# Delta rule of a five-layer kernel: block inverse in 64-column form, three series steps for two joins, small transposes on VectorE

## The reference, cut to what matters

```python
L = jnp.where(strict, jnp.einsum('bhnid,bhnjd->bhnij', k_beta, k) * decay, 0.0)
A = jnp.eye(C, dtype=L.dtype) + L
rhs = jnp.concatenate([v_beta, k_beta * jnp.exp(g)[..., None]], axis=-1)
sol = lax.linalg.triangular_solve(A, rhs, left_side=True, lower=True)
...
def step(state, xs):
    v_new = u_c - jnp.einsum('bhck,bhkv->bhcv', w_c, state)
    o = (jnp.einsum('bhck,bhkv->bhcv', q_c * jnp.exp(g_c)[..., None], state)
         + jnp.einsum('bhij,bhjv->bhiv', a_c, v_new))
    state = state * jnp.exp(g_last)[..., None, None] + jnp.einsum('bhck,bhcv->bhkv', k_dec, v_new)
```

## Time and profile before

| | us |
|---|---|
| median of 3 runs | 2543.03 (2540.28 to 2546.37) |
| the profiled execution | 2544.22 |
| its span, first to last instruction | 2542.4 |
| TensorE busy in the span | 2493.2 |
| VectorE, ScalarE, GpSimd busy | 1619.2, 1032.0, 1181.5 |
| one middle head, from G row to G row | 64.56 |

### The profile page before, as it was taken

The page is one execution under the profiler, slowest core; times in us unless marked ns, Lnnn a source line. Parts: engine busy times, 40 slices in busy tenths (PEclk is TensorE's granted clock), DMA queues, the critical chain, the costliest instruction groups (busy, mean ns, idle before and its releaser), DMA issues.

```text
span 2542.4 us, 31888 instructions
## 1 busy us (share of the span) xinstructions
PE 2493.2 (98%) x11934; PEld 1995.9 (79%) x11934; DVE 1619.2 (64%) x2722; ACT 1032.0 (41%) x1620; POOL 1181.5 (46%) x1447
## 2 busy tenths in 40 slices
PE   8999999999999999999999999999999998999999
PEld 6888878888888877777777788887888776877777
DVE  5644666666666654444343566546998996577876
ACT  3222254444444353333333332224544667454543
POOL 5665643333333265333344366666554533544432
PEclk9999999999999999999999999999999999999999
DMA  3223221111111132222222122232222211221111
GB/s 136 104 100 108 92 79 53 56 54 58 59 67 48 53 111 82 73 73 80 70 83 77 61 100 93 90 108 101 93 98 77 73 46 50 93 93 67 59 67 42
DMA packets 59721, 198.54 MB, mean 78 GB/s; under 512 B 7089, under 2 KB 9649, under 8 KB 59569
## 3 DMA queue, kind: packets, MB, share of 16 engines
q1 hardware_dynamic: 56688, 192.90, 21.7%
q10 hardware_dynamic: 2880, 3.61, 0.6%
HBM read 192.03 MB, written 2.10 MB: 76 GB/s over the span
## 4 chain that ended last, share of the span: by engine, by line
PE 81%; DVE 13%; ACT 4%; issue 2%; DMA 0%; SPq 0%; ACTq 0%; DVEq 0%
PE psum L327 21%; PE psum L329 20%; PE psum L328 20%; DVE psum L935 4%; PE psum L1812 3%; PE psum L2638 1%; PE psum L2623 1%; DVE e_c L935 1%; DVE e_stg L1102 1%; PE psum L2641 1%; PE psum L3099 1%; PE psum L1818 1%; ACT whi L289 1%; PE psum L3076 1%; PE psum L2614 1%
## 5 line engine op out<-in xcount | busy, mean ns | idle before, releaser
L304 POOL TENSOR_TENSOR wlo<-raw,whi 128x256 fp32r<-128x256 f32 x1436 | 1181.0, 855 | 1334.6 <-ACT whi L289 1334.3
L327 PE MATMUL psum<-xh,whi 128*128 128x512 f32 x1800 | 740.7, 412 | 2.6 <-DVE e_stg L1102 1.8
L289 ACT ACTIVATE whi<-raw 128x1024 fp32r<-128x1024 f32 (+1 forms) x369 | 379.4, 1032 | 803.8 <-PE psum L329 779.9
L329 PE MATMUL psum<-xh,wlo 128*128 128x512 f32 x1800 | 705.5, 392 | 0.0
L328 PE MATMUL psum<-xl,whi 128*128 128x512 f32 x1800 | 704.1, 391 | 0.0
L327 PEld LDWEIGHTS psum<-xh,whi 128*128 128x128 f32 x1800 | 340.3, 189 | 78.1 <-issue 13.9
L329 PEld LDWEIGHTS psum<-xh,wlo 128*128 128x128 f32 x1800 | 339.2, 188 | 73.5
L328 PEld LDWEIGHTS psum<-xl,whi 128*128 128x128 f32 x1800 | 340.1, 189 | 69.9 <-issue 6.9
L523 DVE TENSOR_TENSOR xT<-psum,xT 128x512 f32<-128x512 f32 x232 | 156.1, 686 | 159.9 <-PE psum L329 151.9
L615 DVE TENSOR_TENSOR pool_u<-psum,R 128x512 f32<-128x512 f32 x32 | 22.1, 692 | 132.2 <-PE psum L329 132.2
L327 PE MATMUL psum<-pool_y,whi 128*128 128x512 f32 x256 | 99.6, 389 | 0.0
(11 more groups left out here) (555 smaller groups left out, 4425.1 us busy)
## 6 DMA issues: line engine op xcount, KB each, us to landing
raw<-weights_dram SPq DMA_DIRECT2D x329, 512.0 KB, 3.2
raw<-weights_dram SPq DMA_DIRECT2D x40, 384.0 KB, 2.8
xin<-x_dram SPq DMA_DIRECT2D x4, 512.0 KB, 7.8
mla_xrot<-sq ACTq DMA_DIRECT2D x32, 64.0 KB, 2.0
out_dram<-xT SPq DMA_DIRECT2D x8, 256.0 KB, 2.0
g_masks<-gdn_masks_dram ACTq DMA_DIRECT2D x1, 384.0 KB, 3.6
par<-params_dram SPq DMA_DIRECT2D x1, 327.5 KB, 4.2
mwork<-positions_dram ACTq DMA_DIRECT2D x1, 256.0 KB, 2.8
```

Source lines behind the costliest of these rows:

```text
L289: act.activation(whi[:, q, 0:nk * nm * P], raw[:, q, 0:nk * nm * P], ACT.Copy).then_inc(hi_ready[q], 1)
L304: last = pool.tensor_tensor(wlo[:, q, part], raw[:, q, part], whi[:, q, part].bitcast(F32), ALU.subtract)
L327: pe.matmul(gbank(b), whi[:, q, c:c + P], h, start=k == 0, stop=False)
L329: done = pe.matmul(gbank(b), wlo[:, q, c:c + P], h, start=False, stop=k == nk - 1)
```

## The change

For each chunk the diagonal 64 x 64 blocks of all matrices are kept one above the other, 128 rows by 64 columns ("compact"), for use as the moving operand. The left operand of each product stays a 128 x 128 matrix with two diagonal blocks (`left[0..3]`). P (powers) and V (the growing inverse) lie side by side in one tile, so that one weight load serves P*P and P*V. After the 16 x 16 blocks are inverted, X = V*(N above the 16-blocks) is nilpotent, and V + XV + X^2(..) replaces joins 16 and 32. The left operands are made by VectorE transposes of 32-row blocks (`turn`), read from PSUM or SBUF, 30 instructions a head. The 64-join stays.

TensorE's fours a head go from 10 between kk and the 64-join (kq aside) to 7: P2, P4, P8, PV8, X, X2, X2V, of which P2, PV8, X and X2V have 64 columns each. The five groups of transposes in the inverse go.

Other edits: k dec moves from VectorE (one instruction) to ScalarE (four); the k tokens of the next head are made at the end of a head, behind the pieces of `o 3`; the scale beta/|k|^2 is done ahead of d; the Ln of k stands beside the Ln of o, and 1/rms of o is done in the next head behind exp G row (one Ln and one Exp table load less a head); V0 of the next head is projected and taken ahead of z; five tiles are set to zero once. ScalarE's copies of N2, N4, N8 and of U transposed (two of three) go. Pieces: 8 after kk, 3 after each of the next five steps, and for head 0 none after `o 3`.

```diff
-                four_transposes(0, N, "N transposed")
-                more("N transposed")
-                pe.wait_ge(*ve.of(f"{i} Nt"))
-                four(2, NB[:, 0], N, "N2")
+                pe.wait_ge(*ve.of(f"{i} P"))
+                four(2, left[0], Pw, "P2", 64)
...
+                four(0, left[1], PU, "P4")
+                more("P4")
...
+                pe.wait_ge(*ve.of(f"{i} V2"))
+                four(1, left[0], PU, "P8")
+                more("P8")
+                pe.wait_ge(*ve.of(f"{i} V4"))
+                four(2, left[1], V, "PV8", 64)
+                more("PV8")
+                pe.wait_ge(*ve.of(f"{i} V8 turned"))
+                pe.wait_ge(*ve.of(f"{i} above"))
+                four(0, left[0], Nt, "X", 64)
+                more("X")
+                pe.wait_ge(*ve.of(f"{i} X"))
+                four(1, left[2], PU, "X2")
+                more("X2")
...
+                pe.wait_ge(*ve.of(f"{i} V32"))
+                four(2, left[3], V, "X2V", 64)
...
+                if i < H - 1:
+                    k_tokens(pe, i + 1)
                 pe.wait_ge(*ve.of(f"{i} o summed"))
...
+            def turn(dve, i, name, src, dst, spread_out, blocks):
+                for at_row, at_col in blocks:
+                    to = dst[rows(at_col), :, rows(at_row) if spread_out else cols(at_row)]
+                    last = dve.transpose(to, src(at_row, at_col))
+                last.then_inc(*ve.done(f"{i} {name} turned"))
...
+                turn(dve, i, "N", lambda to, of: N[rows(to), :, rows(of)], Nt, False, [(g, g) for g in range(4)])
+                dve.tensor_tensor(left[0][:, :, :], N[:, :, :], over(bd16), ALU.mult).then_inc(*ve.done(f"{i} N 16"))
+                dve.wait_ge(*ve.of(f"{i} N turned"))
+                dve.tensor_tensor(Pw, Nt[:, :, :], over(in16), ALU.mult).then_inc(*ve.done(f"{i} P"))
+                dve.wait_ge(*ve.of(f"{i} P"))
+                dve.tensor_tensor(V, Pw, over(one64), ALU.add).then_inc(*ve.done(f"{i} V1"))
...
+                turn(dve, i, "P2", lambda to, of: half(2)[rows(to), :, cols(of)], left[1], True, [(g, g) for g in range(4)])
+                dve.wait_ge(*ve.of(f"{i} V1"))
+                dve.tensor_copy(Pw, half(2)).then_inc(*ve.done(f"{i} P2"))
...
+                turn(dve, i, "X", lambda to, of: half(0)[rows(to), :, cols(of)], left[2], True,
+                     [(0, 0), (2, 2), (0, 1), (2, 3), (1, 1), (3, 3)])
+                dve.tensor_copy(Pw, half(0)).then_inc(*ve.done(f"{i} X"))
...
+            EARLY = [8, 3, 3, 3, 3, 3, 2, 2, 2, 3]
+            PIECES = {i: EARLY + [2] * 6 + [1] * 4 + [5] for i in (1, 2, 3, 4)}
+            PIECES[0] = [8, 3, 3, 3, 3, 3, 3, 2, 2, 2] + [2] * 6 + [1] * 4 + [0]
```

More of the change, by code:

```diff
@@ L1781, in behind_vector @@
                     yield from take_and_taps(dve, QQ, i + 1)
+                    yield from take_and_taps(dve, V0, i + 1)
                 for d in range(2):
@@ L1940, in work_scalar, with k_dec @@
                 last.then_inc(*ae.done(f"{i} k squares"))
+            def k_dec(act, i):
+                for c in range(NCH):
+                    last = act.activation(kdec[:, c, :], wbank(0)[:, c * P:(c + 1) * P], ACT.Copy,
+                                          scale=gcol[:, 3, c, i:i + 1])
+                last.then_inc(*ae.done(f"{i} k dec"))
+            def work_scalar(act, i):
+                hi = [in_at(i, V1)]
+                if i < H - 1:
+                    hi += [in_at(i + 1, K), in_at(i + 1, QQ), in_at(i + 1, V0)]
+                hi += [z_at(i, 0), z_at(i, 1)]
+                hi += [at["out", h, x] for h, x in halves[i]]
+                if i == 0:
+                    k_squares(act, 0)
+                    act.wait_ge(*ae.of("exp last-G"))
+                    k_dec(act, 0)
+                    act.wait_ge(*ae.of("0 k squares"))
+                    act.activation(rln, ssk, ACT.Ln, bias=bias[:, 0:1]).then_inc(*ae.done("0 ln k"))
                 act.wait_ge(*ve.of(f"{i} d max"))
@@ L2028, in work_vector @@
                     y_before(1)
-                fill("N2")
-                dve.wait_ge(*te.of(f"{i} U2"))
-                dve.wait_ge(*ve.of(f"{i} U1"))
-                dve.tensor_tensor(U[:, :, :], U[:, :, :], chunks(wbank(1)), ALU.add).then_inc(*ve.done(f"{i} U2"))
+                fill("P2")
+                dve.wait_ge(*te.of(f"{i} P4"))
+                turn(dve, i, "P4", lambda to, of: chunks(wbank(0))[rows(to), :, cols(of)], left[0], True,
+                     [(g, g) for g in range(4)])
@@ L2033, in work_vector @@
+                fill("V2")
+                dve.wait_ge(*te.of(f"{i} P8"))
+                turn(dve, i, "P8", lambda to, of: chunks(wbank(1))[rows(to), :, cols(of)], left[1], True,
+                     [(g, g) for g in range(4)])
+                add_to_v(dve, i, chunks(wbank(1))[:, :, 64:P], "V2", "V4")
                 dve.wait_ge(*ae.of(f"{i} E1"))
@@ L2037, in work_vector @@
                 dve.tensor_tensor(A[:, :, :], chunks(wbank(3)), d1[:, :, :], ALU.mult).then_inc(*ve.done(f"{i} A"))
+                dve.wait_ge(*te.of(f"{i} PV8"))
+                add_to_v(dve, i, half(2), "V4", "V8")
+                dve.wait_ge(*ve.of(f"{i} V8"))
+                turn(dve, i, "V8", lambda to, of: V[rows(to), :, cols(of)], left[0], True, [(g, g) for g in range(4)])
                 dve.wait_ge(*ae.of(f"{i} exp G row"))
@@ new lines, in work_vector @@
+                fill("V32")
+                dve.wait_ge(*te.of(f"{i} X2V"))
+                dve.wait_ge(*ve.of(f"{i} V32"))
+                for h, part in enumerate((HI, LO)):
+                    dve.tensor_tensor(U[part, :, part], V[part], half(2)[part], ALU.add)\
+                       .then_inc(*ve.done(f"{i} U" if h else f"{i} U low"))
+                v_beta(dve, i, 0)
+                fill("U")
+                dve.wait_ge(*te.of(f"{i} join"))
+                dve.tensor_copy(Y[LO, :, LO], quarter(0)).then_inc(*ve.done(f"{i} Y"))
@@ L3709 @@
 BIASES = (EPS, EPS * 128, math.pi / 2, 1e-5, EPS * EPS, 128 * EPS * EPS, 64 * EPS)
-GDN_MASKS = ("upper", "-strict lower", "blocks 16", "join 16", "join 32", "join 64")
+GDN_MASKS = ("upper", "-strict lower", "blocks 16", "compact 16", "compact above", "compact identity")
 def constants():
```

257 lines of the change are left out of this document (113 added, 144 removed).

## The result

The changed kernel takes 2579.36 us in the median of four runs (2576.62 to 2580.49), the kernel before 2543.04 beside it: a ratio of 1.014, interval 1.0128 to 1.0152. It is 36 us slower, where 2532 us, 11 us faster, was forecast; the time lies above the range.

The account below looks back on a forecast made before the run. TensorE was taken to bound the kernel, VectorE having least room. Heads 2 to 7 -10.3, head 0 +3.3, head 1 -6.4 made -13.4 us; less 1.2 to the median, plus 2 for small waits: 2532 us, range 2515 to 2556.

Parts of the forecast that it names:

- the head's start: From the sum of o to P: TensorE asks for P at 10.0 us, VectorE has it at 12.1.
- The wait at P2: TensorE waiting for P at a head's start: 2.1 us lost in place of 0.92 at N.
- the clock behind it: TensorE's granted clock after the wait for P: expected to stay at 1.00; a drop costs about 1.4 us.
- the two ends of the stage: Zeroing of new tiles was to fall into an idle VectorE stretch ahead of the stage; no loss was counted.
- three signs of being wrong: Waits at P2 and X2 under 1 us together; transposes at 0.3 or more; TensorE waiting for weights in the stage.
- passes: TensorE's inverse: three fours, five transpose groups and four changes to pieces fewer, saving 4.9 us a head.
- wait at X2: TensorE waiting for X: VectorE ready at 17.2 us after P, TensorE at 15.7, so 1.5 a head.
- P4, P8, PV8: Small waits at the middle products of the inverse, put at nothing; 2 us added in all, also covering v tokens.
- v tokens, sum of o: Waits behind X2 in a head: 0.1 us at v tokens and 0.4 at the sum of o.
- the clock drops: Rival: wait at P 0.2 us longer, clock falling at every head's start, +8.5 us, 2540 us; chance 0.20.
- The slower rival: VectorE transposes are dear: gain gone from 0.30 us each, 2555 us at 0.35, 2565 at 0.40; chance 0.18.
- the narrow rival: 64-column TensorE passes cost by their columns, 0.055 us in place of 0.101: 2527 us; chance 0.08.

Follow-up runs that it names:

- x3_one_turn: Changed kernel with one VectorE transpose in each of eight groups, 22 of 30 a head left out, so the inverse isn't formed; 2534.86 us.
- x2_ktokens: Changed kernel with the next head's k tokens put before the last pieces of a head instead of behind them; 2557.29 us.
- y4_front: y1_together with head 0's VectorE, ScalarE and TensorE work reordered and the pieces of heads 5 to 7 set anew; 2529.28 us, 0.9947 of the kernel before.
- x1_ends: Changed kernel with the five tiles' zeroing moved behind the product z row and head 7's weight copies back before the two silu z; 2569.58 us.
- x6_pieces: Changed kernel with projection pieces moved in heads 1 to 6: 10 for 8 behind kk, 5 for 3 behind X, fewer later; 2574.34 us.
- x4_before_late: Kernel before the change, with 4 pieces after kk and 5 after N transposed in heads 1 to 7, for 7 and 2; 2565.42 us.
- x5_copy_later: Changed kernel with ScalarE's high-half copies of outward weights moved behind the exponential of the next head's G row; 2570.39 us.
- y1_together: Changed kernel with the edits of x1_ends, x2_ktokens and x6_pieces together, head 7 keeping its old pieces; 2546.75 us.

## Why the prediction was wrong

The step that failed is the head's start. The wait at P2 was put at 1.2 us a head over what N's wait had cost, and the clock behind it at nothing; measured were 2.65 and, behind that, 1.6 to 2.9 in each of heads 2 to 7. The chain was the right one, its sizes were not. A second step, that nothing is lost at the two ends of the stage, cost 10 us more. Two of the three signs of being wrong that the prediction names came: transposes of 0.3 or more, and a wait for weights.

A middle head, term by term (before 64.57; after 68.35; predicted 62.9):

| term | predicted | measured |
|---|---|---|
| passes | -4.9 | -3.8 |
| wait at P2, lost time against N's 0.92 | +1.2 | +2.65 |
| clock behind it | 0 | +2.9 |
| wait at X2 | +1.5 | +1.7 |
| P4, P8, PV8 | 0 (2 us in all) | +0.4 |
| v tokens, sum of o | +0.5 | 0 |
| sum | -1.7 | +3.85 |

The head is in fact 3.78 longer.

*The clock*, the largest term, was ruled out by a margin that was no margin. The wait lay between a row that dropped the clock (2.16) and one that did not (1.82). The wait that came, 3.42 idle (2.88 in heads 6 and 7), was beyond both. The drop was priced at 1.4 from a window of 3.4 us, whose granted clock of 0.51 makes it 1.7. It came in every head from 2 to 7; in heads 3 to 5 it held some 6 us and cost 2.9, in the others about 1.6. The rival "the clock drops" had its mechanism right and 8.5 us for it; with the longer wait it was worth some 13.5.

*The chain to P.* Of the 1.5 us that were missed, 0.35 are ScalarE's up to E2 (8.55 for 8.2), 0.28 the four transposes, 0.41 and 0.55 N16 and P beside GpSimd, which the sum had unstretched though the earlier trace rows were read for E2 masked. x3_one_turn shows the last three hang together.

*The transposes.* 0.32 for 0.23. The slower rival named this and the point from which it decides (0.30), and would have had 2532 + 7 x 2.2 = 2547 at 0.32. It was the right rival, with a chance of 0.18, but it priced only the queue. Between P2 and X2, 24 transposes at 0.09 more are 2.2 us: predicted 17.2, in x2_ktokens 19.1. In the kernel after it is 21.3, of which TensorE spends 2.9 on the low clock. That the wait at X2 came out as forecast, 1.6 for 1.5, is partly luck: the queue ran 2 us or more longer, but TensorE came later to X2 too, by the low clock in the kernel after and by small waits at P4, P8 and PV8 in x2_ktokens, where the wait at X2 is 1.6 as well.

*The passes.* 44 fewer a head, and 64 columns at the price of 128, both as forecast; the narrow rival falls. The gain is 3.8: TensorE's small work, from start to start, is 21.9 us in the head before and 18.2 in y4_front's. A four behind a wait costs 0.88 to 0.94 from its start and not 0.81. The 1.7 us a head that the prediction estimates for narrow passes from the formula of the Trainium skill (TensorE: Matmul & The Clock Gate, "Back-to-back issue gap") does not come out of it: 32 passes at 29 ns in place of 56 are an estimate of 0.9. No term of the sum used it.

*The ends*, 10 us. Zeroing "falls into an idle stretch of VectorE": it stood ahead of the intake of z's row, for which TensorE waited 2.4; the G row came 3 us late. The last head's copies were not looked at, though "if TensorE waits for weights anywhere" stood among the signs. x1_ends shows both.

*Head 0.* The wait at the sum of o came as forecast (3.4 for 3.0, clock drop too), the one at P2 at 8.2 for 7.5; with the longer low clock the head got 6.6 dearer and not 3.3. Head 1 lost its wait at P2 as forecast, and gained 3.2 of the 6.4.

So the 36 us between the two traces are 3.0 ahead of head 0's G row, 19.6 in heads 0 to 6, 10.2 from head 7's G row to the end of the stage, and 3.3 behind the stage (from its end to the end of the span 1630.5 us, before 1627.3). The last are the clock's. The sixteen passes of 2 columns in the last layer come four times; in the trace before the clock falls behind two of them, in the trace after behind all four, as here:
```profile
2348.00 2.14 PE L2939 MATMUL psum<-o_mk,o_rr 128*128 128x2 f32 x16 [0.37 <-ACT o_rr L2947]
2350.00 0.78 PE L327 MATMUL psum<-xh,whi 128*128 128x512 f32 x1
```
That is twice more, about 1.6 us each. Over the twelve traces this remainder runs from 1624.9 to 1631.0 with no order by edit. What sets it was not tried.

## What to carry to other kernels

Price the time behind a wait together with the wait: here an idle TensorE of 1.5 to 3.5 us cost between nothing and 2.9 us more in the clock, so the same sum of waits is cheap in pieces of 1 us and dear in one. When work moves from the full engine to the one with room, its place in the chain decides, not the sum of busy time; then set the filler work anew at the new waits, and count, for filler moved forward, how far ahead of its buffers' release it runs. An operation that no trace shows deserves a single measured run before its chain is drawn; here 0.32 in place of 0.23 was worth some 15 us by the prediction's own rival.

## What the hardware showed that was not expected

- VectorE's 32 x 128 transposes in f32 don't overlap: 0.32 us from start to start, 303 ns long from SBUF and 311 from PSUM, while the copy of 256 columns behind them lasts 0.42 and gives way after 0.35.
- The clock after an idle time has no fixed price and no sharp threshold in these runs: behind 2.59 us it fell in heads 4 and 5 and not in 2 and 3 of the same execution, behind 2.07 likewise in x6_pieces, behind 1.53 to 1.58 in heads 2, 5, 6 and 7 and not in 3 and 4 of x3_one_turn, never behind the six of 1.31 in x2_ktokens. Behind 2.99 it held in head 6 of x4_before_late and fell in head 7, and it held behind 3.26 in y4_front. It stayed low 3.4 us behind 2.16, and behind 3.42 now some 3.4 us (head 2) and now some 6 (heads 3 to 5).
- A load of ScalarE's table sometimes runs ahead of the wait of the instruction it is for and sometimes behind it (x5_copy_later: 0.63 us idle for d, then 1.28). In the code the second case has another wait of its own directly ahead; that this is the cause was not tried. The first case, in y1_together, where the load begins before d's maximum does:
```profile
615.61 1.28 ACT L1961 ACT_TABLE_LOAD   x1
616.26 0.43 DVE L2022 TENSOR_SCALAR d<-d 128x512 f32<-128x512 f32 x1
```
